# Spreading a token's slot within its expert block over the 64 slots by a permuted rank

## The reference

```python
e_val, e_idx = lax.top_k(pe, MOE_TOPK)            # MOE_TOPK = 2
expert_id = g_idx[:, None] * MOE_PER_GROUP + e_idx
...
def expert_block(args):
    xblk, e = args
    return (jax.nn.silu(xblk @ w1[e]) * (xblk @ w3[e])) @ w2[e]
...
y = jnp.zeros((N, D)).at[buf_tok].add(yb * buf_w[:, None], mode='drop')
```

## Time and profile before

| | us |
|---|---|
| median of three runs | 1648.42 |
| the three runs | 1643.71, 1648.42, 1649.07 |
| the profiled execution, device time | 1642.52 |
| its span, first to last instruction | 1640.7 |
| layer 0's expert blocks, about | 274 to 772 |
| layer 1's expert blocks, about | 1111 to 1615 |

### The profile page before, as it was taken

How to read it: one execution, slowest core, us unless ns; L and a number is a source line. 1 busy time by engine, 2 the same in 40 slices (tenths; PEclk the granted TensorE clock), 3 DMA queues, 4 the chain that set the end, 5 groups by cost and what they waited for, 6 DMA issues and landing times.

```text
span 1640.7 us, 26411 instructions
## 1 busy us (share of the span) xinstructions
PE 1422.1 (87%) x10070; PEld 884.2 (54%) x10071; DVE 448.7 (27%) x1033; ACT 502.5 (31%) x967; POOL 217.7 (13%) x344
## 2 busy tenths in 40 slices
PE   7998994997888788787699989978988999789993
PEld 5874684554444444444588644765554555445551
DVE  4435635110101010102533499351110111101114
ACT  4516733222122112211322378341222222212222
POOL 4020000121111111111000000101111121112111
PEclk9999996998999899989799999988999999989997
DMA  4313046899999999998432210666999999999995
GB/s 163 104 67 129 2 186 256 324 404 408 412 409 412 406 412 410 408 410 320 138 104 82 86 36 23 250 263 251 413 418 400 351 394 423 417 418 395 402 399 191
DMA packets 69172, 471.48 MB, mean 287 GB/s; under 512 B 11576, under 2 KB 12728, under 8 KB 35840
## 3 DMA queue, kind: packets, MB, share of 16 engines
q1 hardware_dynamic: 54720, 442.93, 67.7%
q0 software_dynamic: 11520, 17.34, 3.2%
q10 hardware_dynamic: 2880, 10.49, 1.7%
HBM read 465.95 MB, written 25.20 MB: 299 GB/s over the span
## 4 chain that ended last, share of the span: by engine, by line
PE 53%; DMA 37%; DVE 5%; issue 2%; ACT 2%; SPq 1%; POOL 0%; DVEq 0%; ACTq 0%; POOLq 0%
DMA w<-in_w 32%; PE bank L386 18%; PE bank L810 17%; PE bank L826 5%; DMA xg<-hn_dram,icol 4%; PE bank L602 2%; PE bank L686 1%; PE bank L698 1%; PE bank L785 1%; PE bank L662 1%; PE bank L651 1%; PE bank L791 1%; DMA YG<-y_dram 1%; PE bank L546 1%; PE bank L728 1%
## 5 line engine op out<-in xcount | busy, mean ns | idle before, releaser
L810 PE MATMUL bank<-w,xT 128*64 128x256 f32 x4480 | 538.5, 402 | 98.0 <-DMA w<-in_w 96.1
L810 PEld LDWEIGHTS bank<-w,xT 128*64 128x64 f32 x4480 | 340.9, 146 | 318.6 <-issue 179.9
L1464 DVE TENSOR_TENSOR hh<-bank,sgate 64x256 f32<-64x256 f32 x140 | 59.6, 426 | 859.7 <-ACT sgate L1060 859.7
L826 PE MATMUL bank<-w,hT 128*64 128x512 f32 x1120 | 255.8, 599 | 0.4 <-ACT hT L1063 0.4
L1060 ACT ACTIVATE sgate<-bank 64x256 f32<-64x256 f32 x140 | 52.5, 375 | 494.2 <-PE bank L810 494.2
L826 PEld LDWEIGHTS bank<-w,hT 128*64 128x64 f32 x1120 | 74.4, 136 | 124.9 <-issue 120.2
L345 ACT ACTIVATE whi<-raw 128x512 fp32r<-128x512 f32 (+1 forms) x112 | 67.8, 615 | 164.9 <-PE bank L386 147.9
L353 DVE TENSOR_TENSOR wlo<-raw,whi 128x512 fp32r<-128x512 f32 (+1 forms) x112 | 77.1, 698 | 139.4 <-ACT whi L345 139.3
L1067 ACT ACTIVATE ysb<-bank 128x512 f32<-128x512 f32 x70 | 41.8, 597 | 238.3 <-PE bank L826 238.3
L1571 POOL DMA_INDIRECT y_dram<-ysb,rcol x70 | 72.7, 1039 | 191.5 <-ACT ysb L1067 187.3
L386 PE MATMUL bank<-whi,hi 128*128 128x512 f32 x224 | 90.2, 403 | 3.5 <-DVE wlo L353 3.5
(11 more groups left out here) (226 smaller groups left out, 1401.6 us busy)
## 6 DMA issues: line engine op xcount, KB each, us to landing
w<-in_w SPq DMA_DIRECT2D x188, 2048.0 KB, 32.8
raw<-in_od_w_in SPq DMA_DIRECT2D x12, 1024.0 KB, 5.1
w<-in_w SPq DMA_DIRECT2D x8, 1024.0 KB, 28.3
raw<-in_ev_w_in SPq DMA_DIRECT2D x6, 1024.0 KB, 5.0
raw<-in_ev_w_out SPq DMA_DIRECT2D x4, 1024.0 KB, 8.0
hn_dram<-HN ACTq DMA_DIRECT2D x8, 512.0 KB, 3.0
YG<-y_dram SPq DMA_DIRECT2D x8, 512.0 KB, 6.1
YG<-y_dram ACTq DMA_DIRECT2D x8, 512.0 KB, 6.2
```

The source lines that it names most:

```text
L810: last = pe.matmul(B[(1, 4)[c]][j * SLOT:j * SLOT + SLOT, 0:HH], xT[:, k, :], W13[s][:, j, k, c * HH:c * HH + HH], start=k == 0, stop=k == ...
L826: last = pe.matmul(B[3][j * SLOT:j * SLOT + SLOT, :], hT[:, k, :], W2[s][:, k, j * 512:j * 512 + 512], start=k == 0, stop=k == FK - 1)
L1464: dve.tensor_tensor(hh[:, c * HH:c * HH + HH].rearrange("q (a p) -> q a p", a=2), B[(1, 4)[c]][SLOT:P, 0:HH].rearrange("q (p a) -> q a p", ...
```

## The change

The constants get one more row of 64 numbers, `slotrank`, and the comparison that makes `slotsel` uses it in place of `iota`. Slot s now takes the token with rank 16 (s mod 4) + floor(s / 4); seen from the token, rank r goes to slot 4 (r mod 16) + floor(r / 16). Ranks 0 to 15 stand in slots 0, 4, 8, ..., 60, ranks 16 to 31 in slots 1, 5, ..., 61, ranks 32 to 47 in slots 2, 6, ..., 62, and the rest in slots 3, 7, ..., 63. The number of blocks, the rows that are gathered and scattered, and every engine's list of instructions stay as they were; the one instruction whose shape differs is the load of the constants behind column 128, now 1243 columns in place of 1179.

```diff
 for _n, _w in (("ident", P), ("blk64", P), ("mean128", P), ("tri", P), ("ones", P), ("triexp", NE + 1),
-               ("thr", 7), ("iota", SLOT), ("dia32", 32), ("tokg", 2 * TT), ("tokv", 2 * TT), ("half", 1), ("eps6", 1), ("eps5", 1),
+               ("thr", 7), ("iota", SLOT), ("slotrank", SLOT), ("dia32", 32), ("tokg", 2 * TT), ("tokv", 2 * TT), ("half", 1), ("eps6", 1), ("eps5", 1),
...
-                dve.tensor_tensor(slotsel[:, :, :], it.unsqueeze(1).broadcast_to([P, 8, SLOT]), bcast(rk[:, 4, :], SLOT), ALU.is_equal)
+                dve.tensor_tensor(slotsel[:, :, :], cst("slotrank").unsqueeze(1).broadcast_to([P, 8, SLOT]), bcast(rk[:, 4, :], SLOT), ALU.is_equal)
...
     put("iota", np.arange(SLOT))
+    put("slotrank", np.arange(SLOT) % 4 * (SLOT // 4) + np.arange(SLOT) // 4)
```

## The result

The changed kernel took 1658.04 us (median of five runs, 1655.13 to 1660.13) against 1648.42 for the kernel before (five runs beside it, 1643.71 to 1649.15). The ratio is 1.0061 with a 95% interval of 1.0048 to 1.0074: slower by some 10 us. The forecast was 1652.2, with a chance of 0.30 for slower by over 0.3%.

What follows compares the result with a forecast made beforehand. Three stretches were held bound by weight arrival, set by the slowest of 16 full DMA engines. 3.8 + 0.3 - 1.3 + 0.3 + 0.15 - 0.15 + 0.1 + 0.6 = +3.8 us on 1648.42 gives 1652.2; 8-in-10 range 1642 to 1661.

Steps and rivals of the forecast that it cites:

- The dealing of slots: Gathers deal neighbouring slot pairs round 16 engines; scatters deal fours round eight engines in each half; chance 0.62.
- The drain: End of layer 0's weight loads: missing DMA share grows from 6.0 to 10 us, half the engines finishing early.
- Rival 1: Four neighbouring slots of a gather share an engine: -17 us in all, 1631.5, drain 3 us; chance 0.08.
- rival 2: Scatters too are dealt in pairs: +15 us, 1663, drain 19 us with DMA gaps before 750; chance 0.12.
- rival 3: Engines get rows as they come, whatever the slot; nothing moves, 1648.5; chance 0.12.
- The quiet gather: Gather of 25 rows without weight traffic should begin fewer packets at once, the rows sitting on 8 engines.
- The lightly loaded engines: They do not run dry: at most 20 us ahead, while loads are asked for 37.1 us before landing.
- Layer 0, +3.8 us: Layer 0's expert blocks: fullest engine goes from 6.7 to 10.5 us over the mean, costing +3.8 us.
- so all of it reaches the end: The stretch from 355 to 762 us waits for weights throughout, so layer 0's whole +3.8 us lengthens the kernel.
- Layer 1, +0.3 and -1.3 us: Layer 1's two weight-bound stretches: fullest engine's excess goes 2.1 to 2.5 us (+0.3), then 3.1 to 1.8 (-1.3).
- The constants: Load of constants grows by 32 KB, 0.08 us at 408 GB/s: +0.1 us at most.
- The gathers, +0.6 us: Where PE binds, blocks of 17 to 32 rows have four rows on the fullest engine, not two: +0.6 us.

Runs made afterwards that it cites:

- e2: Changed kernel with another permutation: ranks 0 to 31 spread over even slots to balance gathers and scatters, wider constants kept; 1642.15 us, ratio 0.9959 to the kernel before.
- g3: The changed kernel, unedited, run again on another occasion for a second profile; 1656.82 us, ratio 1.0048 to the kernel before.
- f1: The change's permutation on the kernel before, its numbers in unused columns of mean128, so constants not widened; 1655.87 us, ratio 1.0032.
- g4: Second occasion of the change's permutation with its numbers in unused mean128 columns, constants not widened; 1656.92 us, ratio 1.0050 to the kernel before.
- f2: Kernel before with the balanced spreading permutation, its numbers in unused mean128 columns, constants not widened; 1643.87 us, ratio 0.9967.
- e4: Changed kernel with a permutation crowding each block's rows on few engines for gather and scatter; 1684.88 us, ratio 1.0238 to the kernel before.
- e3: Changed kernel with slots exchanged by two in every second block, by seven small DVE instructions per router; 1647.90 us, ratio 0.9996 to the kernel before.
- g1: Kernel before with its SBUF constants region 256 bytes longer, nothing more loaded, everything behind it moved; 1647.54 us, ratio 0.9997.
- f4: The kernel before, unedited, run once more for a second profile; 1647.18 us in one profiled run.
- f3: Kernel before with 64 unused columns behind the last constant, 32 KB more to load, no other edit; 1652.99 us, ratio 1.0021.
- g2: Kernel before with 64 unused columns of constants, on a second occasion; 1652.90 us, ratio 1.0033.
- e1: Changed kernel with slotrank holding 0 to 63 in order: constants widened, slots as before; 1652.67 us, ratio 1.0019 to the kernel before.

## Why the prediction was right, and where its sizes were off

**The dealing of slots.** Right, as far as four orders can tell. Gathers go in pairs of slots, scatters in fours. The drain did what it was to do: 9.2 us of missing share against the 10 predicted, with half the engines early. The rules then gave 3.1 us for e2's order (3.4 measured) and a ratio of 0.996 (0.9959 and 0.9967 measured). Rival 1 (fours in the gather) asked for a drain of 3 us and a faster kernel, rival 2 for a drain of 19, rival 3 for none of it; the three fall. The reading of the Trainium skill that stood beside rival 1 (DMA: Bandwidth & Descriptors, section Why a DMA increments its semaphore by 16 and not by 1) falls with it for this gather.

**The quiet gather.** Right. In the stretch in which the gather of layer 0's second block began, to be read beside the first of the earlier trace rows:

```profile
287.22:287.38 0.16, 0.16 (x4) 0.16 (x2) 0.00 (x0) 0.00 (x0) 0.00 (x0) 0.50 1.17 179
```

Here 179 GB/s x 0.16 us = 29 KB = 7 packets began at once, before 9. Two longer stretches say more: by 287.42 it is 164 GB/s x 0.20 us = 33 KB = 8 packets, and then for 0.2 us not one begins.

```profile
287.22:287.42 0.20, 0.20 (x4) 0.20 (x2) 0.00 (x0) 0.00 (x0) 0.00 (x0) 0.50 1.10 164
287.42:287.62 0.20, 0.20 (x4) 0.04 (x2) 0.00 (x0) 0.00 (x0) 0.00 (x0) 0.50 0.00 0
```

Eight engines took a packet each and the other eight had none: the 25 rows sit on 8 pairs.

**The lightly loaded engines.** Right: from 355 to 768.7 the share is 1.00 in the changed kernel, and 1.02 still from 752 to 754, so no engine ran dry before the loads ended.

**Layer 0, +3.8 us.** Right in sign, too small in size. The stretch grew by 3.0 (the changed kernel), 5.8 (g3), 6.9 and 6.5 us (f1, g4) against 425.3; PE's wait for weights there rose by 2.9 in the first profile of the changed kernel, not far above the 1.8 by which the two profiles before differ. In the other three with this order it rose by 5.5 to 10 (77.4, 80.3 and 77.9 from the first `xT` on, against 70.1 and 71.9). The balanced order gave back 3.7 (f2: 4.0) where 3.6 was expected, so the model holds on the side of balance and falls short on the side of imbalance, more so in e4 (22.8 against 13.1). The step that fell short is "so all of it reaches the end", taken as one sum over the layer: the rise of the drain (from 6.0 to between 9.0 and 10.2 us) came as forecast, and layer 0 grew by more than that. e3 shows that equal sums are not enough, since a single load still took 42.35 us; and in e4 long standstills had a lower clock behind them (1.00 at 750, 0.50 at 758).

**Layer 1, +0.3 and -1.3 us.** The second had the wrong sign. In place the permutation made layer 1's blocks about 3 us longer (498.7 and 497.8, against 494.0, 495.7 and g1's 495.5), and the wait for weights was 29.3 and 27.3 us (before 26.1 and 24.1) in place of down. The changed kernel's 29.7 can't be given to the permutation: the wider constants alone have 34.0 and 29.2. I counted the fullest engine over long stretches there too, and a few small blocks were to profit from it. Which block loses the time I did not settle.

**The constants, "+0.1 at most".** This step failed outright. I priced the bytes alone. Alone, they cost 3.5 to 5.4 us, which in the profiles stand in the first blocks (+2.8) and in layer 1 (+4 to +7); both profiled executions lie some 4 us over their kernel's median, as do those of f1 and g3. A cost that I had put at 0.1 us was, alone, as large as the forecast's whole sum. How they cost it stays open.

**The gathers, +0.6 us.** The waits did rise, by 3.6 us in that profile, but not for my reason. In place, with the same four rows on the fullest engine, they were 2.0 and 2.1 us (f4, the kernel before: 3.5), and in f3 and g2 without any permutation 3.4 and 3.9. e3, again with four rows on the fullest engine, has 1.1. The term itself is nothing that these runs can show.

**The sum.** +3.8 us was forecast, +9.6 measured between the medians. The permutation in place accounts for 5.3 (1.0032) to 8.2 us (1.0050). What the constants add to it isn't settled: the change as made had 1.0061 and later 1.0048, the latter beside 1.0050 in place. In layer 0 the two do not quite add up in the profiles. From the first to the last start of `xT`, layer 0 takes 484.2 us before, 487.2 and 487.5 with the wider constants alone, 491.0 and 490.5 with the permutation in place, 490.2 and 492.8 with both. The time fell 1 us above the likeliest case's own range (1645 to 1657), and the verdict that I held likeliest, the same (0.58), did not come. The time lay in the wide range because that reached to a rival that is not what happened. So the mechanism in layer 0 was right, and it is in part luck that the time was inside.

## What to carry to other kernels

Before rows are spread over partitions, find out which partitions share a DMA engine (a quiet transfer's first packets and a stream's drain show it), and count rows per engine for the blocks as they are filled: in a kernel whose weight stream keeps all engines full, the rows that one engine has over the mean can make all loads wait. Here an order made for the pairs and fours gained 0.3 to 0.4%, a plausible one that missed the pairs lost 0.3 to 0.5% by itself, and one that crowded them lost 2.4%. A table that comes with a change is measured apart from it: 256 bytes a partition that nothing read cost 0.2 to 0.3% with the old order, and nothing that showed with the balanced one.

## What was not expected of the hardware

The wider constants' cost is the first: 32 KB more in one load at the start, and a gather almost 300 us later takes over 10 us and lets PE stand, in both profiles of the changed kernel and those of f3 and g2, though not in those of e1, e2 and e3, which have the same widening; while the same addresses in SBUF without the load do nothing. The cause is open, and so is why e2 had none of the cost. e1's two groups of times some 6 us apart need not belong to the constants: f1's twelve times, without the widening, fall in two groups as well (five from 1651.5 to 1652.7, seven from 1655.6 to 1659.9).

The second lies outside the blocks. In layer 1's mixer two profiles of one kernel differ. First the row of the kernel before in its first profile, then in its second (f4), columns as in the earlier trace rows:

```profile
800.00:805.00 5.00, 3.73 (x16) 3.12 (x17) 3.76 (x6) 3.04 (x6) 0.00 (x0) 1.00 0.02 3
```

```profile
800.00:805.00 5.00, 3.94 (x9) 3.14 (x10) 3.54 (x6) 2.20 (x4) 0.00 (x0) 0.53 0.01 3
```

The granted clock stays at 2.4 GHz in one and falls to 1.2 GHz for some us in the other, at the same place of the same program; fewer products are done (9 in place of 16). The mixer's stretch from its first product (L386) to its first scores (L686) is 122.6 us long in the one and 125.4 in the other. It is one reason why single profiles of this kernel can't tell 3 us, and why the 16.7 us between the first two profiles were not the size of the effect.
